# Expert work of a two-layer diffusion step in groups of four tiles instead of pairs, with the spare groups in places 5, 8, 10 and 11 of 12

## The reference, cut to what matters

```python
gate = (one_hot(group) * in_group * group_weight).reshape(lead + (N_EXPERTS,))
hid = silu(einsum('bnd,edf->bnef', h, moe_w1)) * einsum('bnd,edf->bnef', h, moe_w3)
out = einsum('bnef,efd->bnd', hid * gate[..., None], moe_w2)
```

## Time and profile before

| | |
|---|---|
| runs | 1005.09, 1007.42, 1007.64 us, median 1007.42 |
| profiled execution | 1007.64 us, span 1005.5 us |
| PE, matmuls | busy 793.9 us (79%), mean granted clock 0.90 |
| DVE, ACT | busy 479.8 us, 264.0 us |
| HBM | 382.28 MB read; 290.58 MB moved by DMA, mean 289 GB/s |

### The profile page before, as it was taken

The page is one execution under the profiler, slowest core; times in us unless marked ns, Lnnn a source line. Parts: engine busy times, 40 slices in busy tenths (PEclk is TensorE's granted clock), DMA queues, the critical chain, the costliest instruction groups (busy, mean ns, idle before and its releaser), DMA issues.

```text
span 1005.5 us, 18531 instructions
## 1 busy us (share of the span) xinstructions
PE 793.9 (79%) x7937; PEld 531.5 (53%) x7937; DVE 479.8 (48%) x1092; ACT 264.0 (26%) x512; POOL 38.4 (4%) x50
## 2 busy tenths in 40 slices
PE   4599898995846767969877998988697778786985
PEld 3289656873523434535445974677553434353543
DVE  1257987327512333433335798933652342342434
ACT  2356315232100101111125831532221111110113
POOL 4000100000300000000000002000000000000000
PEclk9699989985977989998997997999598898897999
DMA  9944945790899989797793476529068998888881
GB/s 349 337 155 144 399 170 184 298 417 30 340 385 425 387 348 425 285 426 316 311 375 105 163 294 242 176 81 423 7 279 341 386 384 347 347 359 338 355 357 68
DMA packets 73293, 290.58 MB, mean 289 GB/s; under 512 B 8650, under 2 KB 33948, under 8 KB 47868
## 3 DMA queue, kind: packets, MB, share of 16 engines
q1 hardware_dynamic: 69174, 284.39, 72.0%
q0 software_dynamic: 1504, 3.45, 1.0%
q10 hardware_dynamic: 2534, 1.56, 0.5%
HBM read 382.28 MB, written 1.47 MB: 382 GB/s over the span
## 4 chain that ended last, share of the span: by engine, by line
PE 42%; DMA 30%; DVE 15%; ACT 6%; SPq 4%; issue 2%; ACTq 0%; DVEq 0%
DMA ring_b<-in_moe_w 15%; PE bank L1366 14%; DMA ring<-in_moe_w 9%; PE bank L1018 6%; PE bank L1381 4%; PE bank L1252 4%; DVE acc L1576 4%; PE bank L1329 3%; DMA ada<-in_ada_w 3%; SPq L631 3%; DMA ring<-in_ada_w 2%; PE bank L961 2%; DVE hid L1793 1%; PE bank L1294 1%; DMA ring<-in_w_in 1%
## 5 line engine op out<-in xcount | busy, mean ns | idle before, releaser
L1793 DVE SCALAR_TENSOR_TENSOR hid<-sil,gs,bank 64x256 f32<-64x256 f32 x48 | 32.7, 681 | 233.5 <-ACT sil L911 233.5
L1366 PE MATMUL bank<-ring_b,xn 128*32 128x256 f32 x768 | 58.7, 473 | 45.4 <-DMA ring_b<-in_moe_w 45.4
L911 ACT ACTIVATE sil<-bank 64x256 f32<-64x256 f32 x48 | 18.0, 376 | 276.8 <-PE bank L1366 276.8
L1366 PEld LDWEIGHTS bank<-ring_b,xn 128*32 128x32 f32 x768 | 31.5, 135 | 76.7 <-issue 68.4
L1366 PE MATMUL bank<-ring,hT 128*32 128x256 f32 x768 | 51.9, 431 | 22.7 <-DMA ring<-in_moe_w 22.7
L1799 DVE TENSOR_TENSOR y_lo<-bank,y_hi 128x512 fp32r<-128x512 f32 x48 | 33.2, 692 | 74.4 <-ACT y_hi L915 74.4
L1576 DVE SCALAR_TENSOR_TENSOR acc<-zp,convT,acc 128x256 f32<-128x256 f32 x120 | 61.8, 556 | 1.9
L1366 PE MATMUL bank<-ring_b,hT 128*32 128x256 f32 x768 | 48.6, 410 | 14.8 <-DMA ring_b<-in_moe_w 14.8
L1252 PE MATMUL bank<-mixT,ring 128*128 128x256 f32 x256 | 56.9, 381 | 2.9 <-DVE mixT L1646 1.8
L1018 PE MATMUL bank<-x_hi,win_hi 128*128 128x256 f32 x192 | 55.4, 289 | 1.7 <-DVE win_lo L1472 1.7
L1341 PE MATMUL bank<-ST,y_hi 64*128 64x256 f32 x384 | 53.0, 305 | 2.9 <-DVE y_lo L1799 2.9
(11 more groups left out here) (340 smaller groups left out, 1497.7 us busy)
## 6 DMA issues: line engine op xcount, KB each, us to landing
ring_b<-in_moe_w SPq DMA_DIRECT2D x144, 1024.0 KB
ring<-in_moe_w SPq DMA_DIRECT2D x144, 1024.0 KB
ring<-in_ada_w SPq DMA_DIRECT2D x40, 1024.0 KB
ring<-in_w_in SPq DMA_DIRECT2D x14, 1024.0 KB
ada<-in_ada_w SPq DMA_DIRECT2D x4, 2048.0 KB, 23.6
ring<-in_w_out SPq DMA_DIRECT2D x8, 1024.0 KB
wuq<-in_mla_wuq POOLq DMA_DIRECT2D x2, 768.0 KB, 9.9
ring<-in_w_in SPq DMA_DIRECT2D x2, 640.0 KB
```

What stands on the lines that cost most here:

```text
L1366: ins = pe.matmul(B[4][CAP * g:CAP * g + CAP, 0:256], tokens[:, k, c:c + CAP], w[:, g, k * 256:k * 256 + 256], start=(k == 0), stop=(k == ...
L1793: dve.scalar_tensor_tensor(hid[64:128, :].rearrange("s (m p) -> s p m", m=2), sil[64:128, :].rearrange("s (p m) -> s p m", m=2), gs[64:128 ...
```

## The change

Tiles are worked in groups of four (`QUAD`, 128 token slots): 8 base groups and 4 spare ones (numbers 8 to 11), 12 places instead of 24. Spare groups stand in places 5, 8, 10 and 11.

- Weights: the first half of a group (p = 0, two tiles) always uses `ring_b`, the second half (p = 1) `ring`. `ring_b` has two landing semaphores, one for its four up slots and one for its two down slots; with `ring` these are the three rings. SP issues for a group up p0, up p1, down p0, down p1. Up p0 waits for up-projection p0 of the group before (a spare one too), up p1 for its up-projection p1, down for both halves of its down-projection.
- PE: both up-projections (into banks 4 and 7), a quarter of the next batch's gather, combine of the group before with 128 rows, another quarter, two transposes of 128 x 128, down-projection in two halves of 512 columns (banks 5 and 6). A batch is two groups, with the same 256 columns.
- ACT and DVE: sil and hid once for each half, hidT once per group, y_hi and y_lo once for each 512 columns, ST and gates once per group.
- Selection: S is compared with a row 0 to 127 and with positions less the group's first slot (`posq`, one more DVE operation ahead of the first `select`), in parts of 128 columns; the long iota of 1536 becomes two short ones.
- `Y_ORDER` is (0, 1, 2, 3). Vectors for layer 1 go out behind group 1, operands after four up-projections of halves.
- The first input weights of layer 1 wait for all up-projections (slots 0 to 3) and all down-projections (slots 4, 5) of layer 0.

The diff, cut to its core and moved left (removed lines of the functions printed above are mostly left out):

```diff
-ORDER = [0, 1, 2, 3, 16, 4, 5, 17, 6, 7, 18, 8, 9, 19, 10, 20, 11, 12, 21, 13, 22, 14, 23, 15]
...
-BATCH = 4
...
+QUAD = 4 * CAP
+BASE_QUADS = NE // 4
+QUADS = BASE_QUADS + SPARE_TILES // 4
+ORDER = [0, 1, 2, 3, 8, 4, 5, 9, 6, 10, 11, 7]
+assert sorted(ORDER) == list(range(QUADS)) and len(ORDER) == QUADS
+BATCHES = QUADS // 2
+BCOLS = 2 * QUAD
...
+def up_wait(eng, l, i, p):
+    if p == 0:
+        eng.wait_ge(ring_b_up_landed, (l * QUADS + i + 1) * 4 * 16)
     else:
...
+        for slot in range(4):
+            ring_wait(eng, l, slot, unit_loads(l, slot) + i + 1)
+def down_wait(eng, l, i):
+    eng.wait_ge(ring_b_down_landed, (l * QUADS + i + 1) * 2 * 16)
+    for slot in (4, 5):
+        ring_wait(eng, l, slot, unit_loads(l, slot) + i + 1)
...
+                if g < 4:
+                    sp.wait_ge(*up_psum.at(l - 1, 2 * QUADS))
+                else:
+                    sp.wait_ge(*down_psum.at(l - 1, 2 * QUADS))
...
+        def source(name, i, x, held):
+            q = ORDER[i]
+            if q < BASE_QUADS:
+                return a[name][l, 4 * q + x], {}
+            return a[name][l, sp.snap(held[x] % NE)], {"cond": held[x] < NE}
+        def ring_free(i, slot, freed):
+            if i == 0:
+                last = max(g for g in range(units(l)) if g % RING == slot)
+                sp.wait_ge(*unit_done.at(l, last + 1))
+            elif slot in (0, 4):
+                sp.wait_ge(*freed)
+        def up_weights(i, p, held=None):
+            if p == 0 and i > 0:
+                sp.wait_ge(*up_psum.at(l, 2 * i - 1))
+            for g in range(4):
+                src, skip = source(("moe_w3", "moe_w1")[(g // 2) ^ p], i, 2 * p + g % 2, held)
+                if p == 0:
+                    into, landed = ring_b, ring_b_up_landed
+                else:
+                    ring_free(i, g, up_psum.at(l, 2 * i))
+                    into, landed = ring, ring_landed[g]
+                sp.dma_start(into[:, g, :], src.rearrange("(p k) n -> p (k n)", k=KT), **skip).then_inc(landed, 16)
+        def down_weights(i, p, held=None):
+            if p == 0 and i > 0:
+                sp.wait_ge(*down_psum.at(l, 2 * i))
+            for x in range(2):
+                src, skip = source("moe_w2", i, 2 * p + x, held)
+                if p == 0:
+                    into, landed = ring_b, ring_b_down_landed
+                else:
+                    ring_free(i, 4 + x, down_psum.at(l, 2 * i))
+                    into, landed = ring, ring_landed[4 + x]
+                sp.dma_start(into[:, 4 + x, :], src.rearrange("(p k) n -> p (k n)", k=2), **skip).then_inc(landed, 16)
         sp.wait_ge(*mla_ready.at(l, 2))
         sp.wait_ge(*conv_mixed.at(l, 2))
         sp.wait_ge(*cko_psum.at(l, 1))
-        weights(1)
+        up_weights(0, 0)
+        down_weights(0, 0)
         for u in range(ADA_UNITS - 4, ada_units(l)):
             ada_unit(u)
-        weights(0)
+        up_weights(0, 1)
+        down_weights(0, 1)
         sp.wait_ge(*eid_ready.at(l, 1))
-        for i in range(2, PAIRS_E):
...
+        for i in range(1, QUADS):
+            held = None
+            if spare(i):
+                v = 4 * (ORDER[i] - BASE_QUADS)
+                held = [sp.value_load(eid[0:1, v + x:v + x + 1], min_val=0, max_val=NE) for x in range(4)]
+            up_weights(i, 0, held)
+            up_weights(i, 1, held)
+            down_weights(i, 0, held)
+            down_weights(i, 1, held)
+            if i == 1 and l + 1 < L:
                 for dst, src in vectors(l + 1):
...
-        for i in range(PAIRS_E):
...
+        def gathered(b, j):
+            act.wait_ge(*g_psum.at(l, 4 * b + j + 1))
+            act.activation((xn, hT)[b % 2][:, 2 * j:2 * j + 2, :].rearrange("p k t -> p (k t)"), B[6][:, :],
+                           ACT.Copy).then_inc(g_even.sem, 1)
+        def gated(i):
+            for p in range(2):
+                act.wait_ge(*up_psum.at(l, 2 * i + p + 1))
+                if i > 0:
+                    act.wait_ge(*hid_ready.at(l, 2 * i + p - 1))
+                act.activation(sil[64 * p:64 * p + 64, :], B[4 + 3 * p][64 - 64 * p:128 - 64 * p, 0:256], ACT.Silu).then_inc(sil_ready.sem, 1)
+        gathered(0, 0)
+        gathered(0, 2)
+        for i in range(QUADS):
+            gated(i)
+            if i // 2 + 1 < BATCHES:
+                gathered(i // 2 + 1, 2 * (i % 2))
             act.wait_ge(*hidT_psum.at(l, i + 1))
...
+            act.activation(hidT[:, :, :].rearrange("p m t -> p (m t)"), B[5][:, 0:2 * QUAD], ACT.Copy).then_inc(hidT_ready.sem, 1)
+            for half in range(2):
+                act.wait_ge(*down_psum.at(l, 2 * i + half + 1))
+                act.activation(y_hi[:, 512 * half:512 * half + 512], B[5 + half][:, :], ACT.Copy).then_inc(yhi_ready.sem, 1)
...
+        def gather(b, j):
+            if j == 0:
+                pe.wait_ge(*s_ready.at(l, b + 1))
+            if b == 0:
+                if j > 1:
+                    pe.wait_ge(*(g_odd if j % 2 else g_even).at(l, 1))
+            elif b > 1 or j > 0:
+                before = 2 * b + j // 2
+                pe.wait_ge(*(g_even if j % 2 else g_odd).at(l, before + j % 2))
+            bank = B[6 + j % 2] if b == 0 else B[6]
+            for k in (2 * j, 2 * j + 1):
+                for s in range(NS):
+                    for h_part in (h_hi, h_lo):
+                        ins = pe.matmul(bank[:, (k % 2) * BCOLS:(k % 2) * BCOLS + BCOLS], h_part[:, s, k, :], S[:, s, :],
+                                        start=(s == 0 and h_part is h_hi), stop=(s == 1 and h_part is h_lo))
+            ins.then_inc(g_psum.sem, 1)
+        def up(i):
+            tokens = (xn, hT)[i // 2 % 2]
+            if i % 2 == 0:
+                pe.wait_ge(*g_even.at(l, 2 * (i // 2) + 2))
+                pe.wait_ge(*g_odd.at(l, 2 * (i // 2) + 2))
+            for p in range(2):
+                up_wait(pe, l, i, p)
+                if i > 0:
+                    pe.wait_ge(*hid_ready.at(l, 2 * i + p - 1))
+                w = (ring_b, ring)[p]
+                for k in range(KT):
+                    for g in range(4):
+                        c = QUAD * (i % 2) + CAP * (2 * p + g % 2)
+                        ins = pe.matmul(B[4 + 3 * p][CAP * g:CAP * g + CAP, 0:256], tokens[:, k, c:c + CAP],
+                                        w[:, g, k * 256:k * 256 + 256], start=(k == 0), stop=(k == KT - 1))
+                ins.then_inc(up_psum.sem, 1)
         def combine(i):
...
+            last = i == QUADS - 1
+            for k in range(KT):
+                if k % 4 == 0:
+                    pe.wait_ge(*ylo_ready.at(l, 2 * i + k // 4 + 1))
+                for y_part in (y_hi, y_lo):
+                    ins = pe.matmul(B[k // 2][:, (k % 2) * T:(k % 2) * T + T], y_part[:, k * P:k * P + P],
+                                    ST[:, i % 2, :], start=False, stop=last, skip_group_check=True)
+                if last and k % 2:
+                    ins.then_inc(y_psum.sem, 1)
             if not last:
                 ins.then_inc(combined.sem, 1)
         for b in range(4):
             pe.wait_ge(*hhi_ready.at(l, b + 1))
             pe.wait_ge(*hlo_ready.at(l, b + 1))
-        gather(0)
+        for j in range(4):
+            gather(0, j)
         for b in range(4):
             pe.matmul(B[b][:, :], zero[:, 0:P], zero[:, :], start=True, stop=False, skip_group_check=True)
         pe.wait_ge(*rows_ready.at(l, 2))
-        for i in range(PAIRS_E):
...
+        for i in range(QUADS):
+            up(i)
+            if i // 2 + 1 < BATCHES:
+                if i > 0:
+                    pe.wait_ge(*ylo_ready.at(l, 2 * i))
+                gather(i // 2 + 1, 2 * (i % 2))
             if i > 0:
                 combine(i - 1)
...
+            if i // 2 + 1 < BATCHES:
+                gather(i // 2 + 1, 2 * (i % 2) + 1)
+            pe.wait_ge(*hid_ready.at(l, 2 * i + 2))
             for m in range(2):
...
+                ins = pe.transpose(B[5][:, QUAD * m:QUAD * m + QUAD], hid[:, i % 2, m * P:m * P + P], ident)
             ins.then_inc(hidT_psum.sem, 1)
             pe.wait_ge(*hidT_ready.at(l, i + 1))
...
-        combine(PAIRS_E - 1)
+            down_wait(pe, l, i)
+            for half in range(2):
+                if half and i // 2 + 1 < BATCHES:
+                    pe.wait_ge(*g_odd.at(l, 2 * (i // 2 + 1) + i % 2 + 1))
+                for m in range(2):
+                    for x in range(4):
+                        w = (ring_b, ring)[x // 2]
+                        ins = pe.matmul(B[5 + half][CAP * x:CAP * x + CAP, :], hidT[:, m, CAP * x:CAP * x + CAP],
+                                        w[:, 4 + x % 2, m * D + half * 512:m * D + half * 512 + 512], start=(m == 0), stop=(m == 1))
+                ins.then_inc(down_psum.sem, 1)
+        combine(QUADS - 1)
...
+                for j in range(2):
```

(68 more changed lines are left out.)

168 lines of the change are left out of this document (39 added, 129 removed).

## The result

| | before | after |
|---|---|---|
| median of the runs | 1007.33 us (1005.09 to 1007.64, 4 runs) | 1037.55 us (1035.91 to 1042.21, 4 runs) |
| profiled execution, span | 1007.64, 1005.5 us | 1035.91, 1033.8 us |
| granted clock, mean | 0.90 | 0.88 |

The ratio is 1.031, with a 95% interval of 1.027 to 1.035: 30 us slower. The forecast was 1030 us, between 1014 and 1044.

A forecast was written before the change was run, and what follows sets the result against it. The weight stream was taken to bound expert work. Longer stops gave +11.0 us in layer 1 and +9.2 in layer 0, selection and layer ends 2.8: +23.0 on 1007.64, so 1030.6, stated as 1030 us, range 1014 to 1044.

The forecast's parts named there:

- The bound: Expert work in both layers is bound by the weight stream; PE's 1.4 us saved per group was costed at nothing.
- The stops: The weight stream waits behind spare groups for their up-projection: 7.2 us at single places, 22.6 at places 10 and 11.
- How a stop divides: Behind a single spare group: 0.2 + down 3.5 + up 3.5 = 7.2 us without transfer, plus a start.
- A start at 3.8 us: Each start of the weight stream costs 3.8 us; the change turns 17 starts into 8.
- Spare pairs in layer 0, before: Layer 0 of the kernel before: seven stops, each priced at a 3.8 us start and a 0.9 us wait.
- The rate: The weight stream without a stop moves 425 GB/s, 14.8 us per pair of tiles.
- The ends of the layers: From last landing to residual, 4.9 us instead of 4.2: +0.7 us a layer.
- First selection: More, smaller selection steps on the path to the first gather: +0.7 us a layer, from 0.3 to 1.2.
- Skipped loads: SP passes a spare group's skipped issues at 0.6 us each, through by 6.2 us, within the 7.2 us wait.
- (a): Faster, PE sets the time: 976 us; chance 0.08 together with an earlier issue behind spare groups.
- (b): No change: the double spare place costs one stop of 7 to 12 us, not 22.6; 1008 us; chance 0.05.
- (c): Slower still, PE at half clock in the stopped stretches: 3 to 7 us more each, 1052 us; chance 0.12.

## Why the prediction was right, point by point

- **The bound.** Right. Expert work is paced by the weight stream. PE's shorter groups did not show in base groups, whose up-projections still waited for weights (140 us in all), and at places 10 and 11 PE works almost without idle from 954 to 977 while the stream stands still.
- **The stops.** Right in mechanism, which the runs with both orders changed, and with each alone, show. The windows of the changed kernel, behind places 5, 8 and 10 with 11 in layer 1, then the same in layer 0:

```profile
836.00:852.00 16.00, 15.53 (x206) 9.71 (x199) 7.19 (x21) 3.31 (x7) 0.00 (x0) 1.00 0.36 133
908.00:924.00 16.00, 15.53 (x207) 9.69 (x200) 5.40 (x13) 3.31 (x7) 0.00 (x0) 1.00 0.31 115
950.00:980.00 30.00, 29.05 (x387) 17.82 (x386) 10.52 (x24) 5.67 (x12) 0.00 (x0) 1.00 0.16 54
360.00:370.00 10.00, 10.00 (x136) 5.86 (x131) 1.08 (x2) 0.76 (x2) 0.00 (x0) 0.78 0.63 242
425.00:440.00 15.00, 14.35 (x193) 9.81 (x193) 5.34 (x12) 2.60 (x7) 0.00 (x0) 1.00 0.31 115
466.00:497.00 31.00, 29.94 (x394) 19.77 (x393) 11.03 (x25) 5.89 (x13) 0.00 (x0) 1.00 0.17 64
```

Against 425 GB/s they lose 11.0, 11.7, 26.2 and 4.3, 10.9, 26.3 us. The forecast, wait and start together, was 11.0, 11.0, 26.4 and 4.7, 11.0, 26.4. So the sum over the six is the forecast's, 90.4 against 90.5 us, place 5 of layer 0 included, which is as short as a pair's.
- **How a stop divides.** Less well. Without any transfer it is 9 us and not 7.2. PE was not ready when the last weights landed: the up-projection at 830.92 took 5.35 us (granted clock 0.61 in 833 to 836 us) and pushed the down-projection to 840.97, 0.9 us after the stream ended, where I had 0.2. The rest of the 9 us is the time from issue to bytes, which I had put into the start.
- **A start at 3.8 us.** It holds roughly. The first start and the end of the stream lose 1.9 and 2.1 us in layer 1 (747.1 to 750.1 and 1006 to 1009.9 us at 161 and 195 GB/s), 2.0 and 2.2 before. That the run without four spare pairs gained 2.8 us for each and not 4.6 does not speak against it, as said there. The Trainium skill (DMA: Bandwidth & Descriptors, section "Anatomy of one DMA") with its fixed 2.0 us per DMA would have given an estimate of 1016 us, farther from the measured 1037.6 than the sum by the rows; here the measurement decides.
- **Spare pairs in layer 0, before.** This is the term that was most mis-sized. I priced the seven of layer 0 as those of layer 1, at 3.8 + 0.9 us, 32.9 together. They lose 28.1 us, 4.0 each; the eight of layer 1 lose 36.3, 4.5 each. The change takes them away, so it was credited 4.8 us too much. The kernel before, from its first stop behind a spare pair to its last, in layer 0 and in layer 1:

```profile
335.00:501.00 166.00, 131.05 (x1656) 75.45 (x1652) 61.51 (x173) 22.99 (x53) 0.00 (x0) 0.92 0.86 353
766.00:969.00 203.00, 162.33 (x1982) 92.98 (x1977) 74.62 (x210) 27.93 (x64) 0.00 (x0) 0.91 0.85 349
```

- **The rate.** Mis-sized too. I took 425 GB/s for both kernels; over 80 us the changed one moved 421. That adds 14 x 0.14 = 2.0 us in layer 1 and 2.1 in layer 0.
- **Sums.** Lost in layer 1 +14.4 us against the forecast +11.0, in layer 0 +15.0 against +9.2. By these windows the two terms above are 8.9 of the 9.2 us between forecast and measurement. The levels of layer 0 (40.4 and 55.4 us, where I had 36.7 and 45.9) lie higher for both kernels, since they hold the other loads as well.
- **Combine gains nothing.** Right: 16 records 0.12 us apart, 1.9 us.
- **The ends of the layers.** +0.8 in layer 0, as forecast (0.7); +2.2 in layer 1, where the last down-projection began at half clock (records of 1.07 us at 1009.91 instead of 0.62).
- **First selection.** +0.7 forecast. The steps took 0.87 + 1.14 + 0.20 us against 0.61 + 0.88, so +0.7, but the whole way from the residual of layer 0 to the first up-projection of layer 1 grew by 0.2 only.
- **Skipped loads.** I read 0.6 us each from six in 3.64 us. That was a misreading: SP issued four of them by 756.25, then nothing until the down-projection that began at 756.69 was through, and the last two from 758.68 on. It cost nothing, since SP was ready in time either way.
- **Rivals.** (a) and (b) fell: no stop behind an unused group was short. (c), the half clock, holds in small: in the up-projection ahead of each stop of layer 1 and in the last down-projection, not in the stopped stretch, whose granted clock is 1.00.
- **How close it was.** The sum gave 23 us and the medians differ by 30. The span of the profiled execution is 5 us above the forecast's 1028.5; without its early start of 4.7 us it would be 10 us above, and that nearness is luck. The sum of the six stops is no luck, since each of them came out within 0.7 us, but it is closer than the two parts of which each was made.

The first selection of layer 1 in the timeline of DVE, against the earlier trace rows:

```profile
730.91 0.20 DVE L1801 TENSOR_TENSOR posq<-pos,cst 128x48 f32<-128x48 f32 x1
731.15 0.87 DVE L1788 TENSOR_SCALAR S<-row,posq 128x128 f32<-128x128 f32 x4
732.06 1.14 DVE L1792 SCALAR_TENSOR_TENSOR S<-row,posq,S 128x128 fp32r<-128x128 f32 x4
```

## What to carry to other kernels

Where a stream of loads sets the pace, follow a buffer from its free signal back through the program order of the engine that gives it: a stage that moves no bytes can still stand between the stream and its next free slot, and its price is then everything that the engine does between the last landing and that signal. Such an order is held by two queues, the engine's and the issuer's, and changing one of them alone gained nothing here (1041 and 1052 us), while both together took 47 us off. Larger groups lengthen the longest unit that must finish before a slot comes free. Here they beat the kernel before only where unused groups were left out or slots no longer waited for them (988.7 and 985.6 us), and pairs with four spare ones left out reached 982.9; pairs with the same change of both orders were not run, so whether groups are worth having at all stays open.
